# Hybrid decoder trunk: gate tiles, head scores and convolution rows in other places of TensorE's order, squares of q and k on ScalarE, parameters turned after five tiles of x

## What is computed

```
z = rmsnorm(h) @ w_in       # q (8 heads x 64), three k/v pairs (2 x 64 each), branch
                            # gate logits, S5 inputs u (512), merge gates gA, gB (1024 each)
q, ks, kw = rope(rmsnorm_per_head(...))            # kc: per-head norm only
A = bg0 * cmp_attend + bg1 * sel_attend + bg2 * window_attend   # bg = sigmoid of gate logits
    # prompt: causal, T = 256; decode: paged caches of 256 rows; kcmp, vcmp = block MLP
y = S5 scan over u (32 groups, 64 complex states each); B = GLU(gelu(y))
h += (sigmoid(gA) * (A @ w_a) + sigmoid(gB) * B) @ w_o
gate, val = split(rmsnorm(h) @ w_up)
h += (gelu(causal depthwise conv of width 3 (gate)) * val) @ w_down
h += sigmoid(rmsnorm(h) @ w_ple_gate) * (p[layer] @ w_ple)
```

## Time and profile before

| | |
|---|---|
| median of three timed executions | 1193.85 us (1188.97 to 1194.3) |
| the profiled execution's own time | 1188.44 us |
| its span | 1186.8 us |
| mean granted clock of TensorE | 0.989 |
| PE busy | 1120.9 us, 94% of the span |
| DVE busy | 482.5 us, 41% |
| ACT busy | 286.5 us, 24% |
| POOL busy | 156.4 us, 13% |
| mean DMA rate over the span | 137 GB/s |

### The profile page before, as it was taken

How to read it: one execution, slowest core, us unless ns; L and a number is a source line. 1 busy time by engine, 2 the same in 40 slices (tenths; PEclk the granted TensorE clock), 3 DMA queues, 4 the chain that set the end, 5 groups by cost and what they waited for, 6 DMA issues and landing times.

```text
span 1186.8 us, 16480 instructions
## 1 busy us (share of the span) xinstructions
PE 1120.9 (94%) x6314; PEld 921.3 (78%) x6314; DVE 482.5 (41%) x1209; ACT 286.5 (24%) x917; POOL 156.4 (13%) x276
## 2 busy tenths in 40 slices
PE   6998898899999999999999899889999999999995
PEld 4886775678888888888887777666878888888884
DVE  4989615713243222252436854372324223210031
ACT  3434324510111111210344442252112111110021
POOL 6444410002100000005003532000000000000000
PEclk9999899999999999999999999999999999999998
DMA  9553662234645553454645367322444555435430
GB/s 242 172 145 92 205 195 53 72 107 146 165 138 151 142 142 112 123 143 132 205 145 161 97 164 256 77 60 94 142 114 138 155 155 148 120 113 150 139 121 36
DMA packets 239423, 162.23 MB, mean 137 GB/s; under 512 B 25344, under 2 KB 233240, under 8 KB 239208
## 3 DMA queue, kind: packets, MB, share of 16 engines
q1 hardware_dynamic: 229858, 144.45, 42.2%
q0 software_dynamic: 4752, 14.58, 4.3%
q10 hardware_dynamic: 4736, 2.16, 0.7%
HBM read 157.94 MB, written 7.58 MB: 139 GB/s over the span
## 4 chain that ended last, share of the span: by engine, by line
PE 85%; DVE 9%; issue 2%; ACT 2%; DMA 1%; SPq 0%; ACTq 0%; POOL 0%; DVEq 0%; POOLq 0%
PE bank_act L690 39%; PE bank_dve L690 36%; DVE kT L1762 1%; PE bank_dve L1001 1%; PE bank_act L875 1%; PE bank_act L1067 1%; PE bank_o L1081 1%; DVE pcw L1769 1%; PE bank_o L1030 1%; DVE Sf L1751 1%; DVE vpast L1765 1%; DVE vpast L1759 1%; DVE Sf L1766 1%; DVE Sf L1864 0%; DVE mx L1867 0%
## 5 line engine op out<-in xcount | busy, mean ns | idle before, releaser
L690 PE MATMUL bank_act<-xn,ring 128*128 128x264 f32 x1568 | 367.2, 392 | 4.9 <-DVE xn L1727 4.4
L690 PEld LDWEIGHTS bank_act<-xn,ring 128*128 128x128 f32 x1568 | 300.1, 193 | 61.3 <-issue 8.5
L690 PE MATMUL bank_dve<-R,ring 128*128 128x264 f32 x704 | 157.6, 386 | 0.0
L690 PE MATMUL bank_dve<-xn,ring 128*128 128x264 f32 x672 | 156.4, 386 | 0.0
L690 PEld LDWEIGHTS bank_dve<-R,ring 128*128 128x128 f32 x704 | 133.4, 190 | 22.6
L690 PEld LDWEIGHTS bank_dve<-xn,ring 128*128 128x128 f32 x672 | 127.7, 190 | 21.8
L1946 DVE TENSOR_SCALAR PT<-GX,PT 128x264 f32<-128x264 f32 x44 | 18.3, 417 | 200.7 <-ACT GX L1212 200.6
L1212 ACT ACTIVATE GX<-bank_act 128x264 f32<-128x264 f32 x44 | 17.2, 391 | 269.1 <-PE bank_act L690 269.1
L1212 ACT ACTIVATE xn<-hT 128x264 f32<-128x264 f32 x32 | 13.5, 423 | 210.3 <-DVE hT L1965 149.8
L638 POOL DMA_DIRECT2D out_dram<-kall x2 | 1.0, 518 | 466.4 <-ACT kall L1212 466.4
L690 PE MATMUL bank_dve<-sg,ring 128*128 128x264 f32 x256 | 58.6, 388 | 2.9 <-DVE sg L1922 2.9
(11 more groups left out here) (371 smaller groups left out, 1380.2 us busy)
## 6 DMA issues: line engine op xcount, KB each, us to landing
ring<-in_w_up_dram SPq DMA_DIRECT2D x88, 512.0 KB, 5.1
ring<-in_w_in_dram SPq DMA_DIRECT2D x28, 1024.0 KB, 6.0
ring<-in_w_down_dram SPq DMA_DIRECT2D x32, 704.0 KB, 4.6
ring<-in_w_glu_dram SPq DMA_DIRECT2D x16, 512.0 KB, 4.3
ring<-in_w_o_dram SPq DMA_DIRECT2D x8, 1024.0 KB, 5.1
ring<-in_w_ple_gate_dram SPq DMA_DIRECT2D x8, 1024.0 KB, 5.1
PT<-in_cache_cmp_dram SPq DMA_DIRECT2D x64, 64.0 KB, 2.3
ring<-in_w_a_dram SPq DMA_DIRECT2D x8, 512.0 KB, 6.0
```

The source lines that it names most:

```text
L690: ins = pe.matmul(out, lhsT, rhs, start=(k == 0), stop=(k == nk - 1))
```

## The change

PE's order:

- `params_turned` ahead of tile 5 of x instead of tile 2; the layer 0 sum of squares after job 0 instead of job 1.
- Merge-gate tiles: in layer 0 two after job 8 and two after job 14, in layer 1 two after job 5 and two after job 8; two, not four, behind the end states. The chunk of the weights for them is asked for earlier in layer 1.
- The first head score ahead of the compressed scores; head scores 2 and 3 and one gate tile ahead of the decode outputs; one gate tile at units 1, 5, 9 and 13, ahead of `turn_probs(u)` instead of behind it. The wait for the compressed probabilities (`c_prob`) moves into `turn_cmp`.
- The convolution's rows are turned ahead of the wait for `merged` and of all of w_o. The epilogue turns the first half of `hT` for all row tiles, then the second.

ACT and DVE:

- ACT squares q and k (`z_squares`, two instructions for each row tile, after jobs 13 and 14) into scratch of their own; DVE only sums. The Sqrt of the head norms stands at the end of job 15 (layer 0) or 16 (layer 1), ahead of that job's successors. The scratch of the rotary step moves too.
- In the heads stage ACT's order follows PE's; the exponent of the compressed scores comes behind that of unit 0, and that of unit 2 ahead of the copy of the decode outputs. On DVE `scores(0)` comes ahead of the compressed scores.
- On DVE `add_squares` of layer 0 comes ahead of `prep_angles`, tiles 1 and 3 of x ahead of `prep_steps`; `steps(0)` of ACT comes two tiles later.

```diff
-GATES_AT = (8,)
+GATES_AT = ((8, 14), (5, 8))
-SUM_AT = (1, 0)
+SUM_AT = (0, 0)
-GATES_IN_HEADS = (3, 5, 9, 13)
+GATES_IN_HEADS = (1, 5, 9, 13)
+ROOT_AT = (15, 16)
...
@@ PE, prologue
-                    if k == 2:
+                    if k == 5:
                         params_turned(0, dve_bank)
...
@@ PE, jobs loop and behind it
-                    if jobs in GATES_AT:
+                    if jobs in GATES_AT[L]:
                         gates(2)
...
-                gates(4)
+                gates(2)
...
@@ PE, heads
+                head_scores(0)
+
                 banks = [dve_bank() for _ in range(KV)]
...
-                head_scores(0)
                 head_scores(1)
                 gates(1)
...
+                head_scores(2)
+                head_scores(3)
+                gates(1)
                 pe.wait_ge(v_in, L * V_LOADS + V_LOADS)
...
-                pe.wait_ge(c_prob, L + 1)
-                head_scores(2)
-                gates(1)
-                head_scores(3)
...
                 for u in range(2 * H):
                     if u % 4 == 0:
                         turn_cmp(u // 4)
+                    if u in GATES_IN_HEADS:
+                        gates(1)
                     turn_probs(u)
                     if u % 2 == 0 and u + 5 < 2 * H:
                         head_scores(u + 4)
                         head_scores(u + 5)
-                    if u in GATES_IN_HEADS:
-                        gates(1)
...
@@ PE, ahead of w_o
+                pe.wait_ge(conv_in, L * 48 + 48)
+                bank = act_bank()
+                for f in range(KF):
+                    last = pe.transpose(bank[:, 20 * f:20 * f + 20], conv_rows[:, P * f:P * f + P], ident[0:20, 0:20])
+                last.then_inc(act_ready, 1)
                 pe.wait_ge(merged, L * KD + KD)
...
@@ PE, epilogue
-                pe.wait_ge(h_done, DEPTH * KD + KD)
-                for t in range(3):
-                    m = P if t < 2 else NB
-                    for j in range(2):
+                for j in range(2):
+                    pe.wait_ge(h_done, DEPTH * KD + 4 * j + 4)
+                    for t in range(3):
+                        m = P if t < 2 else NB
...
@@ ACT
+                def z_squares(t):
+
+                    m = P if t < 2 else NB
+                    act_.wait_ge(act_freed, base + n[0])
+                    fn(z_sq[t][0:m, 0:QW], z[0:m, t, 0:QW], ACT.Square)
+                    fn(z_sq[t][0:m, QW:896].rearrange("p (j g d) -> p j g d", j=3, g=KV),
+                       z[0:m, t, QW:1280].rearrange("p (j v g d) -> p j v g d", j=3, v=2, g=KV)[:, :, 0], ACT.Square).then_inc(z_squared, 1)
...
+                    if jobs == 13:
+                        z_squares(0)
+                        z_squares(1)
+                    if jobs == 14:
+                        z_squares(2)
+                        if jobs in GATES_AT[L]:
+                            gates(2)
+                    if jobs == ROOT_AT[L]:
+                        act_.wait_ge(hvar_ready, L + 1)
+                        fn(ss[:, 0:2, :], ss[:, 0:2, :], ACT.Sqrt)
+                        fn(ss[0:NB, 2, :], ss[0:NB, 2, :], ACT.Sqrt).then_inc(hstd_ready, 1)
...
-                gates(2)
-                act_.wait_ge(hvar_ready, L + 1)
-                fn(ss[:, 0:2, :], ss[:, 0:2, :], ACT.Sqrt)
-                fn(ss[0:NB, 2, :], ss[0:NB, 2, :], ACT.Sqrt).then_inc(hstd_ready, 1)
                 gates(2)
...
@@ DVE
-            prep_angles(0)
             for k in range(KD):
                 add_squares(0, 0, k)
+            prep_angles(0)
...
-                    tt(w[:, 0:QW].rearrange("p (h d) -> p h d", h=H), zq, zq, MUL)
-                    link(tt(w[:, QW:896].rearrange("p (j g d) -> p j g d", j=3, g=KV), zk, zk, MUL))
-                    link(dve.tensor_reduce(ss[0:m, t, :], w.rearrange("p (h d) -> p h d", d=HD), AX, ADD))
+                    m = P if t < 2 else NB
+                    dve.wait_ge(z_squared, L * 3 + t + 1)
+                    ins = dve.tensor_reduce(ss[0:m, t, :], z_sq[t][0:m].rearrange("p (h d) -> p h d", d=HD), AX, ADD)
```

More of the change, by code:

```diff
@@ L132, in params_taken @@
 def params_taken(L):
-    return 2 if L == 0 else dve_jobs(L - 1, "down", DOWN_PREP[0] + 1 + 1)
+    return 3 if L == 0 else dve_jobs(L - 1, "down", DOWN_PREP[0] + 1 + 1)
 def direct_taken(L):
@@ L143, in qkv_jobs @@
 def qkv_jobs(L, j):
-    return min(j + 1, JOBS) + max(0, j + 1 - LAG[L]) + 4 * (j >= U_AT) + 4 * (L == 0 and j >= B_AT[0]) + 2 * sum(g <= j for g in GATES_AT)
+    return min(j + 1, JOBS) + max(0, j + 1 - LAG[L]) + 4 * (j >= U_AT) + 4 * (L == 0 and j >= B_AT[0]) + 2 * sum(g <= j for g in GATES_AT[L])
 def caches_turned(L, s):
@@ L154, in probs_turned, with weight_chunks @@
 def probs_turned(L, u):
-    return act_jobs(L, "p_probs", u + u // 4 + 2 + sum(v < u for v in GATES_IN_HEADS))
-def weight_chunks():
+    return act_jobs(L, "p_probs", u + u // 4 + 2 + sum(v <= u for v in GATES_IN_HEADS))
+def weight_chunks(L):
     names = []
@@ L165, in weight_chunks @@
             names += [("u", j) for j in range(2)]
[L166 to L170 removed]
+        if 3 * i + 2 in GATES_AT[L]:
+            names += [("gate", GATES_AT[L].index(3 * i + 2))]
+    before_cmp = 5
+    names += [("gate", i) for i in range(len(GATES_AT[L]), before_cmp)]
     names += [("cmp", i) for i in range(2)]
@@ L183 @@
 V_LOADS = 16 * (NB * PAGES + 2)
-CHUNKS = weight_chunks()
-NCH = len(CHUNKS)
+CHUNKS = [weight_chunks(L) for L in range(DEPTH)]
+NCH = len(CHUNKS[0])
 def trunk(nc, A, C, O):
@@ L485, in slot_count @@
         def slot_count(m):
-            return sum(16 * dmas_of(n) for n, _ in (CHUNKS * DEPTH)[m % SLOTS:m + 1:SLOTS])
+            return sum(16 * dmas_of(n) for n, _ in sum(CHUNKS, [])[m % SLOTS:m + 1:SLOTS])
         @block.gpsimd
@@ L984, in layer, with head_scores @@
                     last.then_inc(dve_ready, 1)
+                def head_scores(u):
+                    c, t, g = unit(u)
+                    bank = dve_bank()
+                    n = P * (t + 1)
+                    pe.matmul(bank[:, 0:2 * n], qT[64 * g:64 * g + 64, c, P * t:P * t + P], kT[64 * g:64 * g + 64, :, 0:n],
+                              start=True, stop=True).then_inc(dve_ready, 1)
+                head_scores(0)
                 banks = [dve_bank() for _ in range(KV)]
@@ L1118, in layer @@
                     columns(256, 2, sg[:, 0], KD, dve_bank, dve_ready)
-                    if i == 1:
-                        pe.wait_ge(conv_in, L * 48 + 48)
-                        bank = act_bank()
-                        for f in range(KF):
-                            last = pe.transpose(bank[:, 20 * f:20 * f + 20], conv_rows[:, P * f:P * f + P], ident[0:20, 0:20])
-                        last.then_inc(act_ready, 1)
                     if i == 2:
@@ L1382, in _ @@
                         inputs()
-                    if jobs in GATES_AT:
+                    if jobs in GATES_AT[L] and jobs < 14:
                         gates(2)
@@ L1486, in _ @@
                         small_parameters(L + 1)
-                squares(L, 1, dve_freed, lambda k: dve_jobs(L, "w_o", k + 1), range(4))
-                fn(cvT.rearrange("p f r -> p (f r)"), take(base)[:, 0:20 * KF]).then_inc(act_freed, 1)
-                squares(L, 1, dve_freed, lambda k: dve_jobs(L, "w_o", k + 1), range(4, 6))
+                squares(L, 1, dve_freed, lambda k: dve_jobs(L, "w_o", k + 1), range(6))
                 for k in range(2):
@@ L1843, in _, with scores @@
                 ts(sq4[:, 4:7], sq4[:, 0:3], -1.0, None, MUL).then_inc(s_max, 1)
+                def scores(u):
+                    t = unit(u)[1]
+                    nk = P * (t + 1)
+                    bank = take(base)
+                    if u >= 4:
+                        dve.wait_ge(act_ready, probs_turned(L, u - 4))
+                    stt(S(u), bank[:, 0:2 * nk].rearrange("p (b k) -> p b k", b=2), SCALE,
+                        c_mask[:, SEQ - nk:SEQ].unsqueeze(1).broadcast_to([P, 2, nk]), MUL, ADD).then_inc(dve_freed, 1)
+                    dve.wait_ge(dve_freed, base + n[0])
+                    dve.tensor_reduce(mx[:, u % 4, 0:2], S(u), AX, MAX, negate=True).then_inc(p_max, 1)
+                scores(0)
                 sc = SP_.rearrange("p (t h) n -> p t h n", t=2)
```

84 lines of the change are left out of this document (37 added, 47 removed).

## The result

The changed kernel takes 1160.1 us (median of six executions, 1159.74 to 1160.99) against 1191.57 for the kernel before in the same comparison; the ratio is 0.974, with a 95% interval of 0.9714 to 0.9765. Its profiled execution has a span of 1158.2 against 1186.8, so 28.6 us have to be found. The forecast was 1167, with a sum of 24.0.

A forecast was written before the change was run, and what follows sets the result against it. PE was taken to bound the kernel, busy 1120.9 of 1186.8 us. Gains summing to 24.0 took the profiled 1188.4 to 1164.4; 3 added for spread gave 1167, range 1159 to 1178.

The forecast's parts named there:

- a: Prologue: parameters turned later and sum of squares earlier start the u columns sooner; gain 2.1 us, bounds 1.0 and 3.1.
- b: Layer 0 behind the S5 loop: moved gate tiles cover PE's waits, less ACT stalls; gain 4.1 us, bounds 1 and 7.
- f: Epilogue: first halves of all row tiles go ahead of the last h tile; gain 0.6 us, bounds 0.3 and 1.0.
- e: Ahead of w_o: the convolution's turning fills PE's wait; gain 1.4 us a layer, 2.8 in both.
- part d: Heads, both layers: reordered scores and gate tiles fill PE's waits; gain 5.2 us a layer, 10.4 total, bounds 3.5 and 6 each.
- part c: Layer 1's S5 stage: gate tiles after jobs 5 and 8 cover PE's waits; gain 4.0 us, bounds 1.5 and 5.4.
- an ACT stall that would not come: Range's lower end: no ACT stall in the S5 stages of layers 0 and 1, 4.0 us more gained.
- my 2.6: Layer 0, ahead of the last two gate tiles: PE stalls 2.6 us on ACT's banks, near the middle of 0 and 5.9.
- the first (PE and DVE block each other): Heads loop: gate tiles ahead of turn_probs make PE and DVE wait for each other; 29.8 us lost, 1197; chance 0.04.
- The second (waits move): S5 stages and heads: next waits grow by half of what was won; 9.2 us lost, 1176; chance 0.22.
- The third (ACT's row): S5 stages: ACT's squares, Sqrt and loads cost their upper bound; 4.8 us lost, 1172; chance 0.10.
- The fourth: Clock: new idle stretches over 2 us put PE at half clock in four places; 5 us lost, 1172; chance 0.07.

The follow-up runs named there:

- the filled version of the old order: Changed kernel with the heads stage in the previous kernel's order, plus 11 unread products per layer in PE's idle time there: 1173.63 us.
- the filled version of the changed kernel: Changed kernel plus unread products in PE's idle time: 6 ahead of layer 0's u columns, 2 per layer in the heads: 1159.3 us.

## Why the prediction was right, and where it was not

**Where the time would come from** was right in the main: in the traces all parts went the way forecast, a, b and f within 0.3 of their terms, e within 0.6, and no rival came true as a whole. The trace lost 28.6 instead of 24.0; 3.55 of the 4.6 lie in part d, 0.75 in part c. That the time still lies inside the range, at its lower end, is in part luck: that end was built from an ACT stall that would not come and from a part d of at most 6 in a layer; the stall came, and d went past 6 in both layers (7.77 and 6.18).

**Part d is the term that was mis-sized**: 10.4 forecast, 13.95 measured. Its idle time was right. I had 7.1 of waits less 2.5 of new ones, 4.6; length less busy time is 9.35 before and 4.77 after in layer 0, 4.6. What was missing is busy time: 3.19 in layer 0 and 1.59 in layer 1, where I had 0.6. About 1.6 of it, in both layers, is the order itself, and the rows show how. A head score of 512 columns that stands alone takes as long as two in a row:

```profile
196.46 1.12 PE L1001 MATMUL bank_dve<-kT,aT 64*128 64x512 f32 x2
```

```profile
183.02 1.13 PE L997 MATMUL bank_dve<-kT,aT 64*128 64x512 f32 x4
```

The first is the kernel before, one score (two records); the second the changed kernel, two scores. By shape, these rows sum to 5.6 in layer 1 before and 4.5 after, and the turned probabilities to 8.4 and 7.5. The 0.6 that I counted came from another place, the 1.28 of row 183.70 against 0.70; both are two scores, the two took 0.70 and 0.68 after the change (175.14 and 177.90), and nothing was to be had there. The other 1.6 in layer 0 is clock: in the kernel before it fell in the heads of both layers (184 to 188 and 758 to 761, 1.7 each), after the change in layer 1 only. The profile showed it: the gate tile behind row 183.70 took 5.48 where others took 3.73, and I had it in neither term. That order and clock are two causes is shown by the filled version of the old order (84.34 in both layers at full clock, against 77.93).

**The median** was moved the wrong way by the 3 that I added for the spread. The changed kernel's executions lie within 1.3 us; those of the kernel before within 8.2. The old order of the heads in the changed kernel spread over 9.5, so the order of the heads has to do with it. The spread is one of clock: the executions of the kernel before at 1194 have a mean granted clock of 0.984, those at 1188 to 1189 have 0.989. But the filled version of the old order still spread over 7.6, and what picks the execution in which the clock falls stays open.

**Part b** came out at 3.87 for 4.1 with its pieces in place. ACT's stream at the end of layer 0's S5 stage shows the row that I counted, and PE's wait behind it:

```profile
123.19 1.28 ACT L1217 ACT_TABLE_LOAD   x1
124.48 0.33 ACT L1217 ACTIVATE ss<-ss 128x28 f32<-128x28 f32 x2
```

```profile
125.64 0.26 PE L904 MATMUL bank_act<-c_id,pe_rows 16*128 16x16 f32 x2 [2.26 <-ACT R L1217]
126.13 0.64 PE L912 MATMUL bank_act<-c_id,hs 128*128 128x128 f32 x2 [0.23 <-ACT kall L1217]
...
126.99 8.56 PE L695 MATMUL bank_act<-xn,ring 128*128 128x264 f32 x32
135.39 0.60 PE L926 MATMUL bank_act<-c_id,z 128*128 128x128 f32 x4
```

2.26 + 0.23 for my 2.6, and the two gate tiles at 8.56 instead of 7.3 for a fall that I had put at 0.4 (1.3). That the middle between 0 and 5.9 met it is luck: of the 5.9 only Sqrt and its load (1.61) stood ahead of the copy here; the squares were done at 116.5 and the load back came behind. Sqrt began 1.29 behind the start of its load here as well: the drain that the Trainium skill adds ("ScalarE: Activation LUTs", "What ACT_TABLE_LOAD costs") is not to be seen in this trace either. What the working did not see is that the early Sqrt carries the part: I booked it as a cost, and without it PE waits 4.6 in each layer and the change as a whole loses 12 of its 31.

**Part c** came out at 4.75 for 4.0, and its one cost is right by luck: I had put 1.4 there for Sqrt and its load; 1.28 was measured, but it is the squares of the third row tile that hold the bank. With Sqrt late the wait stays at 1.29, and with the squares on DVE it is 0.23.

**Part a** was right in the trace (2.06; the chain that I named was last, ACT's deviations at 24.39 for my 24.6) and wrong as a gain: putting the old prologue back costs nothing. Half of the 2.06 is not the order either: the changed kernel with the old prologue starts the u columns at 29.93, 1.09 earlier than the kernel before with the same order, in whose one trace the products with `w_in` from 16.22 to 25.59 took 1.1 longer at full clock (9.37 for 8.25); why is not shown. The working did not ask what wait is left ahead of the u columns (3.47) and what the clock does behind it.

**Of the rivals**, the first (PE and DVE block each other) did not come: the loop with the gate tiles ahead is 6.6 faster than with them behind. The second (waits move) holds at most for the prologue. The third (ACT's row) is there at about the forecast's size and no more. The fourth was right that the clock decides some us here, and wrong in its sign: the change gave back more falls than it made (8.5 us lost before, 5.1 after).

**Two of the signs of being wrong** were badly set. The heads stage was to be shorter by 7 to 12, and it was shorter by 14. PE's waits on ACT's banks were not to pass 10: all that ACT ended comes to 11.0 (4.9 before), but only 3.8 of it stands at L904 and L912; much of the rest waits for data that ACT writes.

## What to carry to other kernels

A piece of work that only needs a free bank belongs ahead of the instruction that waits, not behind it: four gate tiles in a layer, put ahead of the turned probabilities instead of behind them, were worth 6.6 us in two layers, 5.5 of them waits. When a cover is moved away from a chain (here gate tiles from ahead of the rotary step), bring the start of that chain forward in the same change, and count both ends together. Undo each part of a change that works: here two of them (the prologue and the squares on ScalarE) earned nothing, and undoing the second gave 3.6 us (in its trace 1.5 in the stretch whose wait went, and more where the clock fell less).

## What the runs showed of the hardware

The granted clock fell to half (0.50, that is 1.2 GHz) behind stretches in which PE was never idle for more than 0.8 us but ran small products: 175 to 184 in the kernel before, and in the filled version of the changed kernel behind 8 us of which PE was busy for 7.8 (0.55 and 0.50 from 734 to 740). The Trainium skill, "TensorE: Matmul & The Clock Gate", "Part 1: The HAM clock gate", has activity release the throttle; the traces agree in so far as 22 unread products kept the clock at 1.00 through both heads stages and made the kernel 8.4 us faster. Which activity is enough, these runs don't tell. The sum of single undoings (22.0 for the heads, 15.2 for the gate tiles of the S5 stage, 12.1 for Sqrt, 3.4 for rows and epilogue) is 52.7, far over the 31.5 of the whole change: the late Sqrt is part of two of them, and each of the first three brought falls of the clock with it.
